# Low parts of the expert weights computed in quarters on VectorE and GpSimd, and GpSimd's low part of U moved to the head of its slot

## The reference

```
g = jax.nn.softmax(top, axis=-1).astype(xc.dtype)
act = jax.nn.gelu(jnp.einsum('nd,nhkd->nhk', xc, expert_u[idx]), approximate=False)
return jnp.einsum('nhk,nhkd->nd', g * act, expert_v[idx])
```

## Time and profile before

| what | value |
|---|---|
| median of the runs | 2034.12 us |
| the profiled execution's own time | 2026.33 us |
| its span, first to last instruction | 2024.9 us |
| mean granted TensorE clock | 0.956 |
| busy: PE / DVE / ACT / POOL | 1847.7 / 1482.8 / 822.7 / 1199.6 us |
| HBM traffic over the span | 242 GB/s |

### The profile page before, as it was taken

How to read it: one execution, slowest core, us unless ns; L and a number is a source line. 1 busy time by engine, 2 the same in 40 slices (tenths; PEclk the granted TensorE clock), 3 DMA queues, 4 the chain that set the end, 5 groups by cost and what they waited for, 6 DMA issues and landing times.

```text
span 2024.9 us, 37848 instructions
## 1 busy us (share of the span) xinstructions
PE 1847.7 (91%) x14571; PEld 1740.4 (86%) x14571; DVE 1482.8 (73%) x2584; ACT 822.7 (41%) x1103; POOL 1199.6 (59%) x855
## 2 busy tenths in 40 slices
PE   7988988798999999999997999998988998989798
PEld 6977764368999999999997999898988998989798
DVE  3669665523589889857765787888768788887977
ACT  4233764423214454457673333343333333333332
POOL 3322222232236888855647787878777778787861
PEclk8999999889999999999998999899999998998999
DMA  5434878652125777756778888988878998998875
GB/s 169 74 106 151 289 253 291 220 219 81 63 98 163 222 225 231 226 185 261 268 289 295 279 302 316 323 311 312 301 279 291 330 318 299 319 318 284 291 276 196
DMA packets 207789, 492.19 MB, mean 243 GB/s; under 512 B 34209, under 2 KB 119266, under 8 KB 187138
## 3 DMA queue, kind: packets, MB, share of 16 engines
q1 hardware_dynamic: 145906, 319.11, 46.4%
q0 software_dynamic: 55296, 167.94, 23.0%
q10 hardware_dynamic: 6416, 2.78, 1.0%
HBM read 449.10 MB, written 40.66 MB: 242 GB/s over the span
## 4 chain that ended last, share of the span: by engine, by line
PE 60%; POOL 13%; DVE 11%; issue 6%; ACT 4%; another core or an unknown queue 3%; DVEq 2%; DMA 1%; ACTq 0%; SPq 0%; POOLq 0%
PE pair L1529 16%; PE pair L1531 16%; PE pair L1530 16%; POOL v_rows L658 6%; POOL picked_a L651 6%; PE pair L1862 3%; PE pair L1674 3%; DVE pair L1428 2%; POOL w_lo L646 2%; DVE act L1470 1%; PE pair L1686 1%; DVEq L1422 1%; PE pair L1726 1%; PE pair L1812 1%
## 5 line engine op out<-in xcount | busy, mean ns | idle before, releaser
L1529 PE MATMUL pair<-x_hi,w_hi 128*128 128x256 f32 (+2 forms) x2224 | 664.9, 299 | 78.1 <-POOL w_lo L646 55.4
L1530 PE MATMUL pair<-x_lo,w_hi 128*128 128x256 f32 (+2 forms) x2224 | 653.8, 294 | 0.7 <-issue 0.7
L1531 PE MATMUL pair<-x_hi,w_lo 128*128 128x256 f32 (+2 forms) x2224 | 652.5, 293 | 0.1
L1529 PEld LDWEIGHTS pair<-x_hi,w_hi 128*128 128x128 f32 x2224 | 434.2, 195 | 83.4 <-POOL w_lo L646 58.8
L1530 PEld LDWEIGHTS pair<-x_lo,w_hi 128*128 128x128 f32 x2224 | 433.7, 195 | 1.9 <-issue 1.7
L1531 PEld LDWEIGHTS pair<-x_hi,w_lo 128*128 128x128 f32 x2224 | 431.9, 194 | 0.7 <-issue 0.7
L658 POOL DMA_INDIRECT v_rows<-in_v_t,at_row x256 | 294.5, 1150 | 148.6 <-DVE pair L1428 80.0
L651 POOL DMA_INDIRECT picked_a<-acts_sparse,at_unit x256 | 325.8, 1273 | 80.3 <-issue 74.9
L1428 DVE SCALAR_TENSOR_TENSOR pair<-v_rows,share,pair 128x1024 f32<-128x1024 f32 x254 | 327.5, 1289 | 25.2 <-issue 3.0
L646 POOL TENSOR_TENSOR w_lo<-w_raw,w_hi 128x1024 fp32r<-128x1024 f32 x106 | 253.1, 2410 | 90.6 <-ACT w_hi L924 90.4
L630 POOL TENSOR_TENSOR w_lo<-w_raw,w_hi 128x2048 fp32r<-128x2048 f32 x22 | 101.5, 4614 | 233.9 <-ACT w_hi L715 233.9
(11 more groups left out here) (234 smaller groups left out, 3775.9 us busy)
## 6 DMA issues: line engine op xcount, KB each, us to landing
w_raw<-in_u_t SPq DMA_DIRECT2D x74, 1024.0 KB, 5.3
v_raw<-in_u_t SPq DMA_DIRECT2D x54, 1024.0 KB
w_raw<-in_v_t SPq DMA_DIRECT2D x128, 256.0 KB
v_raw<-in_v_t SPq DMA_DIRECT2D x128, 256.0 KB
gates<-g_out SPq DMA_DIRECT2D x9, 2048.0 KB, 8.6
g_in<-gates SPq DMA_DIRECT2D x16, 1152.0 KB
v_ring<-in_cache_v SPq DMA_DIRECT2D x64, 256.0 KB, 3.8
v_ring<-in_cache_v POOLq DMA_DIRECT2D x64, 256.0 KB, 4.6
```

The source lines that it names most:

```text
L1529: te.matmul(out, s_hi, m_hi, start=start, stop=False)
L1530: te.matmul(out, s_hi, m_lo, start=False, stop=False)
L1531: return te.matmul(out, s_lo, m_hi, start=False, stop=stop)
```

## The change

The change touches the low parts only. VectorE's low part of a chunk (U and V, second pass) is made by four instructions of 512 elements in place of one of 2048; the semaphore is raised by the last. GpSimd's two halves of a chunk of U (both passes) are each made by two instructions of 512 elements in place of one of 1024, again with the semaphore at the last. And in GpSimd's slots the split stands ahead of all the fetches of the slot, no longer between the two halves of them.

```diff
@@ GpSimd, split_u
                 for j in range(2):
                     cols = slice(P * j, P * (j + 1))
-                    pool.tensor_tensor(lows[w][:, :, cols], by_blocks(u_raw[u_buffer(t)])[:, :, cols],
-                                       highs[w][:, :, cols].bitcast(F32), ALU.subtract).then_inc(u_lo_pool, 1)
+                    for first in (0, KD // 2):
+                        mine = slice(first, first + KD // 2)
+                        last = pool.tensor_tensor(lows[w][:, mine, cols], by_blocks(u_raw[u_buffer(t)])[:, mine, cols],
+                                                  highs[w][:, mine, cols].bitcast(F32), ALU.subtract)
+                    last.then_inc(u_lo_pool, 1)
@@ GpSimd, the slots of the second pass
-                mine = rows_added_at(slot)
-                for k in mine[:len(mine) // 2]:
-                    fetch_ahead(k)
                 if slot + 1 < STEPS and not on_vector(STEPS + slot + 1):
                     split_u(STEPS + slot + 1)
-                for k in mine[len(mine) // 2:]:
+                for k in rows_added_at(slot):
                     fetch_ahead(k)
@@ VectorE, split_u
-                v.tensor_tensor(lows[w], by_blocks(u_raw[u_buffer(t)]), highs[w].bitcast(F32), ALU.subtract)\
-                    .then_inc(u_lo_vector, 2)
+                for q in range(4):
+                    mine = slice(2 * q, 2 * q + 2)
+                    last = v.tensor_tensor(lows[w][:, mine], by_blocks(u_raw[u_buffer(t)])[:, mine],
+                                           highs[w][:, mine].bitcast(F32), ALU.subtract)
+                last.then_inc(u_lo_vector, 2)
@@ VectorE, split_v
-                v.tensor_tensor(lows[w], by_blocks(v_raw[c % 2]), highs[w].bitcast(F32),
-                                ALU.subtract).then_inc(v_lo_done, 1)
+                for q in range(4):
+                    mine = slice(2 * q, 2 * q + 2)
+                    last = v.tensor_tensor(lows[w][:, mine], by_blocks(v_raw[c % 2])[:, mine],
+                                           highs[w][:, mine].bitcast(F32), ALU.subtract)
+                last.then_inc(v_lo_done, 1)
```

## The result

The changed kernel is slower: 2115.73 us (median of 4 runs, 2112.38 to 2119.35) against 2036.53 us for the kernel before (4 runs, 2033.16 to 2039.93). The ratio is 1.0389, 95% interval 1.0362 to 1.0417. The forecast was 1963 us in a range of 1930 to 2010. The profiled execution has a span of 2113.6 us, with TensorE's mean granted clock at 0.939; before it was 2024.9 us and 0.956.

A forecast was written before the change was run, and what follows sets the result against it. PE was taken to bound the first pass and GpSimd the second; slots falling from 14.43 to 13.3 us save 72 us, less 1 in the first pass: 2034.1 - 71 = 1963 us, range 1930 to 2010.

The forecast's parts named there:

- The hold and the quarters: Second pass: VectorE's quarters let GpSimd's fetches in, cutting their excess from 136 us to 20 to 25.
- rival 3: Quarters on VectorE do not let GpSimd's fetches in; no change, 2034 us, chance 0.05.
- 2 to 4.9: Hold of VectorE by each GpSimd split in the second pass: could rise from 2 to 4.9 us.
- row 1155.85: Earlier trace: VectorE's L1470 took 3.94 us, kept out over both GpSimd instructions; grounds for expecting it over all four.
- The first pass: GpSimd's quarters there are mostly hidden: +1 us taken, the pass within 2 us of 470.
- PE's waits for GpSimd: Second pass: PE's wait for GpSimd's low part, 51.9 us before, falls under 10 us.
- Rival 4: GpSimd's split ahead of the fetches starves VectorE of rows in every third slot: slower, 2064 us, chance 0.06.
- two signs of being wrong: VectorE showing waits for rows, or PE waiting for VectorE's low parts for tens of microseconds.
- the sum: Second-pass slot falls from 14.43 to 13.3 us: 72 us over 64 slots, less 1 in the first pass, 71.
- stalls like the 14.7 us of 'issue' will stay: Second pass: PE stalls that no event ends remain, each with its stretch at the lower clock.
- the 13.3 us for a slot: Second-pass slot time after the change, half a microsecond over PE's floor, from 14.43 us.
- the step on the split at the head: GpSimd's split moves ahead of the slot's fetches: SyncE freed some 5 us earlier, rows fetched 5 us later with room.

The follow-up runs named there:

- set 1: First set of follow-up runs, four variants beside the kernel before (2004.74 us); none had slow stretches (TensorE instruction starts repeatedly 0.33 to 2.2 us apart).
- set 3: Third set of follow-up runs, with the changed kernel and three variants run again beside the kernel before, which took 2029.03 us.
- vec_quarters_head: Changed kernel with GpSimd's low part of U left in two whole instructions, the split still ahead of the fetches: 2092.6 us, 1.029 of the kernel before.
- rests_behind: Changed kernel with three rests (drains and memsets) on GpSimd behind the last fetch pair of slots without a split: 2309.88 us, 1.1373 of the kernel before.
- small_rows: Changed kernel with every row fetch cut to a quarter of its bytes, part of the output differing: 1955.32 us, 0.9747 of the kernel before.
- vec_quarters: Kernel before with only VectorE's low parts in quarters: 1971.98 us, 0.983 of the kernel before; run again later, 2015.94 us, 0.9937.
- units_between: Changed kernel with one unit fetch behind each quarter of GpSimd's split and the row fetches behind the last: 2018.1 us, 0.9891 of the kernel before.
- set 5: Fifth set of follow-up runs, two variants of the changed kernel's fetches beside the kernel before, which took 2040.36 us.
- small_rows_again: Second run of the changed kernel with row fetches cut to a quarter of their bytes: 2106.35 us, 1.0387 of the kernel before.
- after_third: The changed kernel as it is, run a third time: 2092.96 us, 1.0323 of the kernel before.
- set 2: Second set of follow-up runs, the changed kernel again with variants beside the kernel before (2029.85 us), on the same chip as the first set.
- vec_quarters_paced: Kernel before with VectorE's low parts in quarters and GpSimd rests between fetch pairs of slots without a split: 2603.64 us, 1.2797 of the kernel before.
- paced_fetches: Changed kernel with fetch pairs behind each split quarter and GpSimd rests between pairs in the other slots: 2608.6 us, 1.2829 of the kernel before.

## Why the prediction was wrong

**Right.** *The hold and the quarters.* The excess of the 506 fetches over 0.945 us fell from 136 to 258.2 + 245.4 - 478.2 = 25 us, forecast 20 to 25; rival 3 is refuted by this. Four quarters on VectorE take 2.48 to 2.53 us (2.49 forecast). VectorE is kept out over all four of GpSimd's instructions:

```profile
1203.19 5.04 DVE L1473 TENSOR_TENSOR act<-act,g_in 128x288 f32<-128x288 f32 x2
1208.16 2.48 DVE L1490 TENSOR_TENSOR x_lo<-v_raw,x_hi 128x512 fp32r<-128x512 f32 x4
L1473 DVE TENSOR_TENSOR act<-act,g_in 128x288 f32<-128x288 f32 x128 | 141.1, 1131 | 106.1 <-ACT act L954 88.6 <-issue 17.5
...
L1418 DVE TENSOR_TENSOR share<-share,picked_a 128x8 f32<-128x8 f32 x32 | 5.3, 166 | 0.0
```

The two L1473 take 5.04 us where two alone take 0.82; the mean rose from 634 to 1131 ns, an excess of (1131 - 450) x 128 = 87 us, 4.4 for each of 20 splits, in the upper half of "2 to 4.9". By the sentence of the Trainium skill ("SBUF — State Buffer", "SBUF: two separate sides") that whichever of the two starts first has the shared pair of ports for one whole instruction, VectorE could have come in after 1.3 us. The row goes against it, as row 1155.85 did in the earlier trace rows. L1418, on the other hand, is held no more (166 ns, from 540). *The first pass* and *PE's waits for GpSimd* (4.2 us, under 10 forecast) came as said. *Rival 4* did not come: L1428 has 23.2 us of idle time in 254 instructions (25.2 before). So neither of the two signs of being wrong that the prediction named came: VectorE hardly waits for rows, and PE waits 0.8 us for VectorE's low parts in the second pass. It was wrong by something that it had named no sign for.

**The step that failed** is in the sum: "stalls like the 14.7 us of 'issue' will stay", and with it the 13.3 us for a slot. They did not stay, they grew from 29 to 122 us at the three products, and the slot became 16.2 us (14.8 before, the 60 full slots by gelu). I had read these stalls as a constant of the kernel. They follow the very quantity that the change raises: how many fetches GpSimd issues in a short time. Two steps of the change each took away something that had kept it low. VectorE's long splits had held about every fifth fetch (98 of 506 took over 1.1 us), for up to 2 us; and the split in the middle of a slot had cut its eight fetches in two, while at the head it leaves all eight together, and those of the next slot behind them (15 in 18.8 us in the stretch shown). In the step on the split at the head I counted only the room that the fetches have to be late, not that they then come close together. The quarters alone gained 1.7% in set 1 and only 0.6% in set 3, where they had 81 us of slow stretches against 49 to 57 in the kernel before. Both together lost 3%: vec_quarters_head (1.029) is nearly the whole of the loss. The place alone did no harm in set 1 (1.0004); what it does alone where slow stretches come was not run.

The rows to see it in were there. Before, the "issue" idle time had its stretches nearly only (11 of 12) in the slots in which VectorE holds the fetches least, and most of them ended about 2 us after the last of GpSimd's fetches in a row. I took the largest row of PE's waits as the whole story and never looked at what went on around the second.

**Shown and not shown.** Shown: that the loss stands or falls with the place of the split once VectorE's low parts are in quarters (1.029 against 0.9965 in one set), and the slow stretches with it (192 against 89 us); that they go away with a quarter of the fetches of units left out (0.944) and not with three quarters of the bytes of rows; that spacing the fetches within GpSimd's slots leaves 24 us of them. Not shown: which count, over how long a time, sets them off (rests_behind has the runs and hardly any stretches); whether fetches of rows and of units count alike; by what path GpSimd's issue of an indirect fetch reaches TensorE; and what kept it away in set 1. The changed kernel was not run in a set like the first, so whether it gains there is open; small_rows had the same runs of fetches there and no slow stretch.

Of the kernels that compute all of the output, two gain most against the kernel before: vec_quarters, by 1.7% in set 1 and 0.6% in set 3, and units_between, by 1.1% in set 5. They were not run in one set, and the intervals 0.9912 to 0.9962 and 0.9839 to 0.9943 overlap, so which of the two is better is open.

## What to carry to other kernels

A hold or a wait may be a brake that something else depends on: before you remove it, ask what will then run at full rate, and look for the places in the trace of before where it already does. A small row of stalls with no releaser needs its place in time read, beside every engine's queue, before it is called a constant. And an experiment in which all variants win says something about the set of runs before it says something about the variants: run the changed kernel in it too.

## What the runs showed of the hardware

- In runs of indirect fetches that GpSimd issues 1.25 us apart, mostly with 7 or 8 in the last 10 us, TensorE can fall to one instruction in 0.7 us, in most cases until 1 to 3 us after the last fetch of the run. The size of the rows has hardly a part in it: it comes with rows of 1 KB for each partition as with rows of 4 KB (192 us in small_rows_again, 178 in after_third). Such runs do not always bring it (8 us in rests_behind, none in small_rows in set 1).
- Whether this happens can change between two sets of runs. On one chip four kernels had none of it in set 1 and four had it in set 2, and the kernel before took 2004.74 and 2029.85 us; small_rows took 1955.32 and 2106.35 us, on two chips.
- Two drains and two small memsets on GpSimd behind an indirect fetch left it idle for up to 10.0 us (vec_quarters_paced), and for 385 us in 80 such rests in the window of paced_fetches.
- GpSimd's instructions that follow each other at once hold VectorE's instruction with two inputs in SBUF out over all of them (two take 5.04 us, 0.82 alone), but between VectorE's quarters a fetch of GpSimd gets in (means of 1009 and 981 ns, from 1273 and 1155).
